# Attention by pairs of heads in row and column halves of TensorE, with fixed windows of 256 grid keys

## What is computed

```python
def _context_attention(q, k, v):
...
        s = jnp.einsum('bqhd,bkhd->bhqk', qi, k).astype(jnp.float32) * scale
        p = jax.nn.softmax(s, axis=-1).astype(v.dtype)
        return jnp.einsum('bhqk,bkhd->bqhd', p, v)

def _neighbourhood_attention(q, k, v, k_ctx, v_ctx, rpb):
...
        s_win = jnp.einsum('bqhd,bjkhd->bhqjk', q_r, k_band).astype(jnp.float32) * scale + bias[None]
        s_win = jnp.where(col_mask[:, None, :], s_win, NEG)
        s_ctx = jnp.einsum('bqhd,bchd->bhqc', q_r, k_ctx).astype(jnp.float32) * scale
        s = jnp.concatenate([s_win.reshape(B, H, GRID_W, n_win), s_ctx], axis=-1)
        p = jax.nn.softmax(s, axis=-1).astype(v.dtype)
...
        return (jnp.einsum('bhqjk,bjkhd->bqhd', p_win, v_band)
                + jnp.einsum('bhqc,bchd->bqhd', p_ctx, v_ctx))
```

## Time and profile before

| | us |
|---|---|
| median of 3 runs (lowest, highest) | 664.93 (664.69, 665.69) |
| the profiled execution | 664.67 |
| its span | 662.9 |
| PE busy in it | 579.1 (87%) |
| DVE busy | 422.5 (64%) |
| ACT busy | 293.3 (44%) |
| PE's share of the chain that ended last | 73% |

### The profile page before, as it was taken

How to read it: one execution, slowest core, us unless ns; L and a number is a source line. 1 busy time by engine, 2 the same in 40 slices (tenths; PEclk the granted TensorE clock), 3 DMA queues, 4 the chain that set the end, 5 groups by cost and what they waited for, 6 DMA issues and landing times.

```text
span 662.9 us, 9135 instructions
## 1 busy us (share of the span) xinstructions
PE 579.1 (87%) x2988; PEld 455.2 (69%) x2988; DVE 422.5 (64%) x671; ACT 293.3 (44%) x487; POOL 184.2 (28%) x201
## 2 busy tenths in 40 slices
PE   3888996999999899999999999369999999999800
PEld 3346884898898367666878888237888888888700
DVE  3419456587304955644555355786999899999528
ACT  5207133131211245434553033225888888888400
POOL 2030222211000300000021000052787887883300
PEclk9877998999999999999999998779999999999965
DMA  9990030304354208502417533447958669997757
GB/s 331 387 306 33 0 128 16 128 1 142 108 212 154 103 1 297 211 1 96 162 62 288 221 128 127 158 180 305 368 225 329 241 213 397 383 362 293 262 223 276
DMA packets 41602, 130.23 MB, mean 196 GB/s; under 512 B 6140, under 2 KB 6156, under 8 KB 35296
## 3 DMA queue, kind: packets, MB, share of 16 engines
q1 hardware_dynamic: 32176, 109.62, 44.3%
q0 software_dynamic: 8400, 19.63, 8.3%
q10 hardware_dynamic: 992, 0.55, 0.3%
HBM read 121.35 MB, written 18.38 MB: 211 GB/s over the span
## 4 chain that ended last, share of the span: by engine, by line
PE 73%; DVE 15%; DMA 5%; ACT 2%; issue 2%; POOL 1%; SPq 1%; ACTq 1%; DVEq 0%; POOLq 0%
PE bank L1375 17%; PE bank L1377 17%; PE bank L1376 17%; PE bank L1546 3%; DMA big<-w_ada 3%; PE bank L1665 2%; PE bank L1508 2%; PE bank L1524 2%; PE bank L1491 2%; PE bank L1371 2%; DVE hu L1085 2%; PE bank L1596 2%; PE bank L1510 1%; DVE big_r L923 1%; PE bank L1412 1%
## 5 line engine op out<-in xcount | busy, mean ns | idle before, releaser
L1375 PE MATMUL bank<-big_r 128*128 128x512 f32 (+1 forms) x264 | 101.2, 383 | 3.3 <-DVE hu_r L955 3.3
L1144 DVE TENSOR_TENSOR big_r<-big,big_r 128x2048 fp32r<-128x2048 f32 x38 | 87.0, 2290 | 5.8 <-ACT big_r L793 5.7
L793 ACT ACTIVATE big_r<-big 128x2048 fp32r (+1 forms) x38 | 72.9, 1918 | 30.3 <-issue 24.8
L1376 PE MATMUL bank<-big_r 128*128 128x512 f32 x200 | 79.7, 399 | 0.0
L1377 PE MATMUL bank<-big_r,hu_r 128*128 128x512 f32 x160 | 64.0, 400 | 0.0
L1377 PE MATMUL bank<-big_r 128*128 128x512 f32 (+1 forms) x176 | 63.7, 362 | 0.0
L1375 PEld LDWEIGHTS bank<-big_r 128*128 128x128 f32 x264 | 54.6, 207 | 9.9 <-issue 3.4
L1376 PEld LDWEIGHTS bank<-big_r 128*128 128x128 f32 x200 | 42.6, 213 | 6.6
L548 POOL TENSOR_TENSOR small<-small 128x8 f32<-128x8 f32 (+1 forms) x15 | 21.5, 1431 | 92.4 <-DVE small L981 58.0
L620 POOL COPY small<-small 128x1 uint32 x19 | 32.3, 1699 | 26.1 <-ACT rs L848 18.5
L739 ACT ACTIVATE xt<-xt,small 128x256 f32<-128x256 f32 (+1 forms) x32 | 18.0, 561 | 47.3 <-DVE small L1073 47.0
(11 more groups left out here) (269 smaller groups left out, 1369.5 us busy)
## 6 DMA issues: line engine op xcount, KB each, us to landing
big<-w SPq DMA_DIRECT2D x32, 1024.0 KB, 7.8
big<-w_ada SPq DMA_DIRECT2D x12, 2048.0 KB, 15.1
hu<-w SPq DMA_DIRECT2D x16, 1024.0 KB, 8.1
big<-w_in SPq DMA_DIRECT2D x5, 2048.0 KB, 9.5
big<-slot_out SPq DMA_DIRECT2D x10, 512.0 KB, 7.4
big<-w_out SPq DMA_DIRECT2D x2, 2048.0 KB, 10.5
x_rows<-big SPq DMA_DIRECT2D x5, 512.0 KB, 2.6
h_rows<-vr SPq DMA_DIRECT2D x5, 512.0 KB, 2.6
```

Source lines behind the costliest of these rows:

```text
L793: nc.scalar.activation(w13_hi[p][:, v, :], w13_raw(v, par), ACT.Copy).then_inc(w13_hi_ready, 1)
L1144: V.tensor_tensor(w13_lo[p][:, v, :], w13_raw(v, par), w13_hi[p][:, v, :].bitcast(F32), ALU.subtract).then_inc(w13_lo_ready, 1)
L1375: T.matmul(out, lhs[0], rhs[0], start=start, stop=False)
L1376: T.matmul(out, lhs[0], rhs[1], start=False, stop=False)
```

## The change

Steps become 20 pairs of heads of one tile. The two heads of a pair are computed in the two row halves for the scores (their banks differ) and, with v as the weights and the transposed probabilities streaming, in the two column halves for the values, so that the output comes out turned. Every latent tile uses one window of 256 grid keys (`WIN_FROM`), inner ones beginning half a tile early, so that a head's 512 scores lie in one bank; one add-and-max on DVE (with zeros for the cached keys) and one exponential on ACT serve a head. For the shifted windows POOL makes three copies of v shifted by 64 partitions (`v_half`, six DMAs). `bm` has 6 pieces instead of 7, of which the last two are made during tile 1 and 2. Since the output is turned, the division becomes a product with the reciprocals spread over 512 columns and transposed by PE (`sums_inverse`, `sums_T`, `copy_sums`); `att_T` goes, also the one behind the first output product. The first group of the map moves to pairs 0 to 2, the second to 12 to 14; attention's `keep_busy` matmuls go, and three are added behind the last `columns`. Of the rewritten functions only new lines are shown; the old ones stand in the listing above.

```diff
+WIN_FROM = (0, P // 2, 3 * P // 2, 2 * P)
+WIN = 2 * P
+PIECES = 6
+LEFT_EDGE, INNER, RIGHT_EDGE = 0, 2, 4
...
-        probs = [xt[:, s * 640:(s + 1) * 640] for s in range(2)]
-        win = [xt[:, 1280 + s * 384:1280 + (s + 1) * 384] for s in range(2)]
+        probs = [xt[:, s * 512:(s + 1) * 512] for s in range(4)]
...
-        pT = [po[:, s * 640:(s + 1) * 640].rearrange("p (j n) -> p j n", j=5) for s in range(2)]
-        o_rows = [po[:, 1280:1280 + AW]] * TILES
+        pT = [po[:, s * 512:(s + 1) * 512].rearrange("p (j n) -> p j n", j=4) for s in range(2)]
+        v_half = [po[:, 2 * AW:3 * AW], po[:, 3 * AW:4 * AW], hu[:, HEADS * PIECES * P:HEADS * PIECES * P + AW]]
...
-        ada_first = (5, 20)
-        turn_at = {14: 0, 18: 1, 30: 2, 34: 3}
-        busy_at = {0: 0, 1: 0, 2: 0, 3: 0, 4: 0, 16: 1, 32: 3, 39: 4}
-        ada_at = {first + k: (g, k) for g, first in enumerate(ada_first) for k in range(KD)}
-        ada_ends = {first + KD - 1: g for g, first in enumerate(ada_first)}
...
+        ada_at = {m: (g, ks) for g, first in enumerate((0, 3 * PPT)) for m, ks in (
+            (first, range(0, 3)), (first + 1, range(3, 6)), (first + 2, range(6, KD)))}
+        ada_ends = {2: 0, 3 * PPT + 2: 1}
+        bias_pieces = ((LEFT_EDGE, 2, "from"), (LEFT_EDGE + 1, 4, "right"), (INNER, 1, "upper"), (INNER + 1, 3, "lower"),
+                       (RIGHT_EDGE, 0, "left"), (RIGHT_EDGE + 1, 2, "upto"))
+        bias_at = {0: (0, 1), 1: (2, 3), 2: (4, 5), 3: (6, 7), 7: (8,), 8: (9,), 9: (10,), 10: (11,)}
...
+            for i in range(3):
+                for half in range(2):
+                    pool.dma_start(v_half[i][half * 64:half * 64 + 64, :],
+                                   v_sb[64 - half * 64:128 - half * 64, 1 + i + half, :]).then_inc(v_half_in, 16)
+            nc.gpsimd.memset(no_bias, 0.0).then_inc(no_bias_ready, 1)
...
+            def softmax(m):
+                t = m // PPT
                 nk = key_tiles(t)
+                act.wait_ge(nmax_ready, m + 1)
...
+                for n in (2 * m, 2 * m + 1):
+                    src = probs[n % 4] if t else banks[n % 4][:, 0:P]
+                    nc.scalar.activation(probs[n % 4][:, 0:nk * P], src, ACT.Exp, bias=nmax[:, n % 4:n % 4 + 1],
+                                         accum_out=sums[:, t % 2, n % HEADS:n % HEADS + 1]).then_inc(exp_done, 1)
...
+            def copy_sums(t):
+                act.wait_ge(sT_done, t + 1)
+                nc.scalar.activation(catT[:, 0:4, t * P:(t + 1) * P], banks[7][:].rearrange("p (j n) -> p j n", n=P),
+                                     ACT.Copy).then_inc(sT_copied, 1)
+            def round_att(t):
+                act.wait_ge(att_ready, t + 1)
+                ts = slice(t * P, (t + 1) * P)
+                nc.scalar.activation(cat_r[:, 0:4, ts], att[:, :, ts], ACT.Copy).then_inc(att_hi, 1)
...
+            softmax(0)
+            softmax(1)
+            for m in range(PAIRS):
+                tile_ends = m % PPT == PPT - 1
+                copy_pT(m)
+                if tile_ends:
+                    copy_sums(m // PPT)
+                if m + 2 < PAIRS:
+                    softmax(m + 2)
+                if tile_ends:
+                    round_att(m // PPT)
+                if 11 <= m < 15:
+                    round_sg(m - 11)
+                if 16 <= m < 20:
+                    split_hi(("out", 0), m - 16, wout_hi)
...
+                for n in (2 * m, 2 * m + 1):
+                    if t == 0:
+                        V.tensor_reduce(m_all[:, n % 4:n % 4 + 1], banks[n % 4][:, 0:P], X, ALU.max).then_inc(win_ready, 1)
+                        continue
+                    at_ = (n % HEADS * PIECES + bias_of(t)) * P
+                    bias = bass.AP(bm.tensor, bm.offset + at_, [bm.ap[0], (NO_BIAS_AT - at_, 2), (1, WIN)])
+                    V.tensor_tensor_reduce(out=probs[n % 4].rearrange("p (c n) -> p c n", c=2),
+                                           in0=banks[n % 4][:].rearrange("p (c n) -> p c n", c=2), in1=bias,
+                                           scale=1.0, scalar=-3e38, op0=ALU.add, op1=ALU.max,
+                                           accum_out=m_all[:, n % 4:n % 4 + 1]).then_inc(win_ready, 1)
+                dve.wait_ge(win_ready, 2 * m + 2)
+                V.tensor_scalar(nmax[:, pair], m_all[:, pair], -1.0, None, ALU.mult).then_inc(nmax_ready, 1)
...
+            def copy_pT(m):
+                w = key_tiles(m // PPT)
+                dve.wait_ge(pT_done, 2 * m + 2)
+                if m:
+                    dve.wait_ge(pv_done, m)
+                V.tensor_copy(pT[1][:, 0:w, :], banks[5][:, 0:w * P].rearrange("p (j n) -> p j n", n=P)).then_inc(pT_dve, 1)
+            def sums_inverse(t):
+                dve.wait_ge(exp_done, HEADS * (t + 1))
+                link(V.reciprocal(rsum, sums[:, t % 2]))
+                if t:
+                    dve.wait_ge(sT_done, t)
+                V.tensor_copy(r_rows.rearrange("p (h d) -> p h d", h=HEADS),
+                              rsum.unsqueeze(2).to_broadcast((P, HEADS, HD))).then_inc(sums_ready, 1)
             def normalise(t):
+                dve.wait_ge(sT_copied, t + 1)
+                dve.wait_ge(pv_done, PPT * (t + 1))
+                ts = slice(t * P, (t + 1) * P)
+                V.tensor_tensor(att[:, :, ts], banks[6][:].rearrange("p (j n) -> p j n", n=P), catT[:, 0:4, ts],
+                                ALU.mult).then_inc(att_ready, 1)
...
+            largest(0)
+            largest(1)
+            for m in range(PAIRS):
+                t, tile_ends = m // PPT, m % PPT == PPT - 1
+                if tile_ends:
+                    sums_inverse(t)
+                copy_pT(m)
+                if m + 2 < PAIRS:
+                    largest(m + 2)
+                if tile_ends:
+                    normalise(t)
+                if m % PPT == 0 and t:
+                    rest_att(t - 1)
+                for i in bias_at.get(m, ()):
+                    bias_piece(i)
+                if m in ada_ends:
+                    ada_group(ada_ends[m])
+                if 12 <= m < 16:
+                    rest_sg(m - 12)
+                if 16 <= m < 20:
+                    split_lo(("out", 0), m - 16, (wout_hi, m - 15), wout_lo)
...
+            for _ in range(3):
+                keep_busy(banks[4][:])
...
+            def scores(m):
+                t, hp = m // PPT, m % PPT
+                if m >= 2:
+                    pe.wait_ge(exp_done, 2 * m - 2)
+                keys = [kT[:, hp, 0:P]] if t == 0 else [kT[:, hp, P + WIN_FROM[t - 1]:P + WIN_FROM[t - 1] + WIN], ckT[:, hp, :]]
+                for j, k in enumerate(keys):
+                    for a in range(2):
+                        lo = HD * a
+                        ins = T.matmul(banks[(2 * m + a) % 4][:, j * WIN:j * WIN + k.shape[1]],
+                                       qT[lo:lo + HD, hp, t * P:(t + 1) * P], k[lo:lo + HD], start=True, stop=True)
+                ins.then_inc(scored, 1)
...
+                m, a = n // 2, n % 2
                 pe.wait_ge(exp_done, n + 1)
+                if m:
+                    pe.wait_ge(pT_dve if a else pT_act, m)
+                for j in range(key_tiles(m // PPT)):
+                    ins = T.transpose(banks[4 + a][:, j * P:(j + 1) * P], probs[n % 4][:, j * P:(j + 1) * P], ident[:])
+                ins.then_inc(pT_done, 1)
...
+            def values(m):
+                t, hp = m // PPT, m % PPT
+                pe.wait_ge(pT_act, m + 1)
+                pe.wait_ge(pT_dve, m + 1)
+                if hp == 0 and t:
+                    pe.wait_ge(att_ready, t)
+                if m == 2 * PPT:
+                    pe.wait_ge(v_half_in, 16 * 6)
+                lat = [v_sb[:, 1 + i, :] for i in range(4)]
+                v = [v_sb[:, 0, :]] if t == 0 else list((lat[0:2], v_half[0:2], v_half[1:3], lat[2:4])[t - 1]) + [
+                    cv[:, 0, :], cv[:, 1, :]]
+                for j, rows_ in enumerate(v):
+                    for a in range(2):
+                        lo = (2 * hp + a) * HD
+                        ins = T.matmul(banks[6][HD * a:HD * (a + 1), hp * P:(hp + 1) * P], rows_[:, lo:lo + HD],
+                                       pT[a][:, j, :], start=(j == 0), stop=(j == len(v) - 1))
+                ins.then_inc(pv_done, 1)
...
+            def sums_T(t):
+                pe.wait_ge(sums_ready, t + 1)
+                pe.wait_ge(rows_ready, 1 if t < 3 else 2)
...
             pe.wait_ge(cache_in, 64)
+            scores(0)
+            scores(1)
             pe.wait_ge(sgu_out, TILES)
-            scores(0)
-            for n in range(len(steps)):
-                if n + 1 < len(steps):
-                    scores(n + 1)
-                if n in ada_at:
-                    ada_part(*ada_at[n])
-                if n in busy_at:
-                    if busy_at[n]:
-                        pe.wait_ge(aT_lo_ready, busy_at[n])
-                    keep_busy(banks[7][:])
```

(20 more changed lines are left out.)

250 lines of the change are left out of this document (60 added, 190 removed).

## The result

| | us |
|---|---|
| after, median of 4 runs (lowest, highest) | 625.65 (624.18, 627.05) |
| before, median of 4 runs beside them | 664.81 (664.01, 665.69) |
| ratio, with its 95% interval | 0.941 (0.939 to 0.944) |
| the profiled execution of after, its span | 627.05, 625.3 |

The account below looks back on a forecast made before the run. PE, busy in nearly every slice, was taken to bound the kernel. From 664.7 us, attention -28.2, transposes behind it -0.6 and keep-busy matmuls at the start -1.0 gave 634.9, forecast as 635.0, range 621 to 649.

Parts of the forecast that it names:

- PE's pair: Latent tile, PE work for two heads: transposes 0.97, scores 0.95, values 0.95, sum 2.9 us where 6.06 stood.
- The loop of two pairs: Attention, scores(m+2) to scores(m+4): ScalarE's queue order sets 6.9 us, 3.45 a pair; fifteen pairs after pair 4 take 51.8.
- Rival 1: Attention pairs: PE alone limits, copies not in the way, 2.95 us a pair; 627.5 us in all. Chance 0.12.
- Additions behind the exponentials: Attention pairs: attention roundings 0.6 x 3, a gating rounding 0.7, late bias pieces 0.8; 3.3 us added.
- Clock elsewhere in the stage: Attention outside the entry: one more stretch at half clock, 2.0 us.
- Entry: Attention's start: w_ada wait, 3.0 us charged for the clock, VectorE series of 10.3, values 0.9; pair 4 ends at 245.2.
- Tail: From the second map's end to attention's end: 24.0 us instead of 18.2, with ScalarE waiting 1 us for w_out.
- Start: Before the projections: three keep-busy matmuls fill PE's wait; between -2.4 and +0.6 us, taken as -1.0.
- Behind attention: Behind the first output product: the last tile's four transposes go, -0.6 us; what follows is shifted whole.
- The two rules: Skill rules against the change: transposes do not count as PE-busy like other matmuls; column tiling excludes Fast Weight Load.
- rival 3: Attention: clock stays at half, PE becomes the bound, 670 us, chance 0.05; for half of the stage 652, 0.07.
- rival 2: Values: column halves load weights in turn, 3.9 a pair, 642 us, chance 0.12; row halves too, 654.5, 0.05.

Follow-up runs that it names:

- later remainders: Changed kernel with VectorE's four rest pieces of w_out's first half one pair later each than ScalarE's rounding of them: 624.17 us.
- values head by head: Changed kernel with each pair's values issued as four key tiles of the even head, then four of the odd, instead of alternating: 632.02 us.
- roundings later as well: Against the kernel with remainders one pair later and first map group in pairs 1 and 2: ScalarE's w_out roundings one pair later, remainders one more; 622.35 us.
- the keep-busy matmuls at the entry: Changed kernel with four 512-column keep-busy matmuls ahead of the first map part in pair 0, where PE waits for w_ada: 628.24 us.

## Why the prediction was right, and where it was off

The ledger of the profiled executions (664.67 to 627.05):

| step | forecast | measured |
|---|---|---|
| start, to the last gating tile's end (three keep-busy matmuls) | -1.0 | -2.2 |
| gating's end to the end of pair 4 | 28.8 | 26.6 |
| from there to the second map group's end | 45.3 | 40.4 |
| tail | 24.0 | 25.8 |
| attention (sum of three, less 126.3) | -28.2 | -33.5 |
| behind it | -0.6 | -1.9 |

- **PE's pair.** Transposes 1.02, scores 1.06, values 1.03 against 0.97, 0.95, 0.95; 3.12 without waits instead of 2.9. The overlap of both kinds of halves, taken from neighbours, is shown by taking the halves away; it is close to full.
- **The loop of two pairs.** 3.45 forecast, 3.41 and 3.42 measured, with the wait where it was put, on ScalarE's copy; and turning that queue round removed it. Rival 1 (2.95, 627.5 us) gave nearly the measured total, by a wrong mechanism: PE does wait in most pairs, and even without that wait seven pairs took no less.
- **The step that failed: "Additions behind the exponentials", 3.3 us, and "Clock elsewhere in the stage", 2.0 us.** Both were put on top of the loop. Without them the forecast from pair 4 to the second map group's end is 40.0 us (45.3 less 5.3), and 40.4 were measured. By queue, all four late bias pieces and one rounding of a tile fell in the seven pairs up to 265.49 (24.79 us against 24.15 for the loop alone), a second rounding and the gating roundings in the three pairs with the map, and the third rounding of a tile in the tail. ACT and DVE had gaps in each pair and most of that work went into them. The clock stayed at 1.00 from 240.7 to 281.1; it fell in the tail instead. That is 4.9 of the 7.9 us by which the profiled execution lies below the forecast (the median is 1.4 lower still).
- **Entry.** The landing of `w_ada` (5.87 us after the gating instead of 5.6), the half-clock stretch and the long series on DVE came as forecast. The half clock cost 2.4 instead of 3.0: 18 passes in 4.46 us where 24 take 2.78. Six parts were charged behind the landing, but six of their 48 passes had run before it. And the series from the scores of pair 4 (DVE took them up at 230.20) to the pair's end at 240.70 was 10.5 instead of 11.2.
- **Tail.** 24.0 against 25.8. The arrival of `w_out` was right: ACT waited 0.49 (forecast 1). The walk had DVE's remainders ahead of its copies at their own 1.2 us. What it missed is that they wait there for ACT (2.54 and 2.53), and that the clock would fall over it.
- **Start.** By the thirteenth instruction of the projections after is 1.3 us ahead of before, by the mechanism named; the forecast's 1.0 was sound. The other 0.9 of the 2.2 came later, in work that was not changed, and is luck: the first scores of like kernels range from 212.0 to 216.5.
- **Behind attention.** The four transposes were a small term. The larger part is the clock, below.
- **The two rules.** From 240.7 to 281.1 transposes were a third of PE's time in a plain pair (1.02 of 3.1 us), and the granted clock was 1.00 throughout. So the rule of the Trainium skill (TensorE: Matmul & The Clock Gate, Part 4: PE-mode transpose) did not become rival 3 here. That transposes count in full isn't shown either, since scores and values stand between them. Loads of a column half took 135 to 150 ns in the mean, sixteen passes of both heads 1.03 us, and with the halves taken away a pass of 128 columns 0.12 where one of 256 took 0.24. Whatever column tiling excludes by the Trainium skill (TensorEngine Tiling (Array Packing), Restrictions and Gotchas), no load was exposed; rival 2 (642) did not come, and its second part (row halves in turn on 256 columns) needed the halves to be taken away by hand, which gave 639.88.
- Rival 3 had a share: 3.4 us of the entry and 10.3 of the tail ran at half clock. It cost some 6 us (2.4, and 3.4 by the run with later remainders), not 20, as PE waited in much of that time anyhow.

## What to carry to other kernels

When a loop is held by a queue on one engine, small additions mostly go into the gaps of the engines beside it (0.4 us measured here for 3.3 charged): add to the forecast only what lies in the loop's own chain. A postponed side task should not stand in a queue ahead of the work that the bottleneck waits for, least of all if it waits for a third engine itself; moving DVE's remainders by one pair shortened the tail by 6.2 us; moving them and ACT's roundings by one more gained nothing. Put passes whose operands are on their way behind everything that is ready: the map group one pair later shortened the entry by 3.8 us, of which some 2.5 were its own and the rest the place of a half-clock stretch.

## What the runs showed of the hardware

- Two heads' passes in different column halves overlap even when issued one head after the other, but only for half of them: the second head's first pass started after the first head's fourth of eight (rows of values head by head). For the eight passes of the scores in row halves the order cost nothing.
- The rest, some 319 us of unchanged work, came in two groups. It was 318.4 to 319.0 in seven kernels and 320.0 to 320.5 in five more (and 319.8 in the thirteenth, roundings later as well, which has a wait of its own there). In every kernel the unchanged part ends with some 29 us at half clock. It has other stretches before that; in after, windows of them are

```profile
374.40:377.90 3.50, 3.50 (x6) 1.44 (x6) 2.33 (x3) 0.44 (x2) 0.65 (x2) 0.51 0.37 150
384.70:401.80 17.10, 6.81 (x23) 3.25 (x24) 14.35 (x60) 2.20 (x3) 4.00 (x8) 0.50 0.13 50
408.60:412.00 3.40, 3.40 (x13) 2.99 (x12) 2.98 (x3) 1.08 (x2) 1.51 (x4) 0.50 1.06 422
```

and in before

```profile
408.60:415.40 6.80, 6.80 (x20) 4.80 (x21) 4.85 (x6) 1.15 (x2) 0.64 (x2) 0.50 0.23 95
422.20:439.30 17.10, 6.72 (x23) 3.24 (x24) 14.36 (x60) 2.37 (x3) 3.85 (x7) 0.50 0.05 14
446.10:449.50 3.40, 3.40 (x13) 3.01 (x13) 2.92 (x3) 1.09 (x2) 1.44 (x4) 0.50 1.01 424
```

24.0 and 27.3 us. The kernels with the short rest all had 24.0 us in these stretches, those with the long rest 27.3, whatever their attention looked like; the thirteenth had 24.0. PE was busy throughout the 3.3 us of difference, so half of it, about 1.7 us, is an estimate of its cost, and the two groups lie that far apart. Of the 1.9 us that after gained behind attention, some 1.7 is thus a matter of where these stretches fall, and a kernel that gains or loses 1.7 us there has not been shown to be faster or slower. With the scatter of the runs, two medians of this kernel closer than about 3 us are not told apart, as the keep-busy matmuls at the entry show.
